# Decoder block on one core: the first norm's root by Ln, Exp and a Newton step, the second ada row in one dot, and the activation's low half ahead of the weight's

## What is computed

```python
mod = silu_c @ w_ada[l] + b_ada[l]                  # 6 vectors of 2048
sh1, sc1, g1, sh2, sc2, g2 = jnp.split(mod, 6, axis=-1)
h = modulate(rms_norm(x, norm1_w[l]), sh1, sc1)     # h*(1+sc1)+sh1
proj = h @ w_in[l]
```

## Time and profile before

| what | value |
|---|---|
| median of 3 runs | 2343.6 us (2343.4 to 2343.84) |
| the profiled execution's own time | 2344.19 us |
| its span | 2342.4 us |
| TensorE busy | 2320.1 us (99%) |
| VectorE busy | 1256.4 us (54%) |
| ScalarE busy | 721.7 us (31%) |
| GpSimd busy | 90.7 us (4%) |
| granted TensorE clock, mean | 0.998 |
| transfers | 327.21 MB, mean 140 GB/s; 388 and 410 GB/s in the first two of 40 slices |

### The profile page before, as it was taken

How to read it: one execution, slowest core, us unless ns; L and a number is a source line. 1 busy time by engine, 2 the same in 40 slices (tenths; PEclk the granted TensorE clock), 3 DMA queues, 4 the chain that set the end, 5 groups by cost and what they waited for, 6 DMA issues and landing times.

```text
span 2342.4 us, 28296 instructions
## 1 busy us (share of the span) xinstructions
PE 2320.1 (99%) x10432; PEld 1891.1 (81%) x10432; DVE 1256.4 (54%) x1577; ACT 721.7 (31%) x1013; POOL 90.7 (4%) x59
## 2 busy tenths in 40 slices
PE   8999999999999999999999999999999999999998
PEld 5578888887888888888888888888888888888887
DVE  8989888866666675633333333333333333333354
ACT  3333333344445322421321321322222222222233
POOL 0011112101010000000000000000000000000000
PEclk9999999999999999999999999999999999999999
DMA  9965767622223573222222222222222222222222
GB/s 388 410 240 205 260 244 261 232 81 81 81 79 106 201 282 122 99 96 93 99 99 98 90 98 98 92 98 97 98 98 90 98 98 96 99 92 98 99 90 99
DMA packets 89575, 327.21 MB, mean 140 GB/s; under 512 B 8625, under 2 KB 9137, under 8 KB 89521
## 3 DMA queue, kind: packets, MB, share of 16 engines
q1 hardware_dynamic: 89232, 326.34, 38.8%
q10 hardware_dynamic: 290, 0.16, 0.0%
HBM read 322.27 MB, written 4.19 MB: 139 GB/s over the span
## 4 chain that ended last, share of the span: by engine, by line
PE 92%; DMA 3%; DVE 2%; issue 1%; ACT 0%; POOL 0%; ACTq 0%; POOLq 0%; DVEq 0%
PE bank L478 29%; PE bank L482 29%; PE bank L479 29%; DMA prob<-ada 3%; PE bank L689 1%; PE bank L655 1%; DVE w_lo L1209 1%; DVE ada_sb L1215 0%; PE bank L680 0%; PE bank L594 0%; PE bank L523 0%; PE bank L535 0%; PE bank L672 0%; PE bank L827 0%; PE bank L633 0%
## 5 line engine op out<-in xcount | busy, mean ns | idle before, releaser
L478 PE MATMUL bank<-act_hi,w_hi 128*128 128x512 f32 x2016 | 790.7, 392 | 0.3 <-ACT w_hi L885 0.3
L479 PE MATMUL bank<-act_lo,w_hi 128*128 128x512 f32 x2016 | 785.3, 390 | 0.0
L885 ACT ACTIVATE w_hi<-raw 128x1024 fp32r<-128x1024 f32 x393 | 415.0, 1056 | 835.4 <-PE bank L482 825.8
L1209 DVE TENSOR_TENSOR w_lo<-raw,w_hi 128x1024 fp32r<-128x1024 f32 x393 | 496.3, 1265 | 293.6 <-ACT w_hi L885 280.1
L482 PE MATMUL bank<-act_hi,w_lo 128*128 128x512 f32 x2016 | 498.2, 389 | 0.1
L478 PEld LDWEIGHTS bank<-act_hi,w_hi 128*128 128x128 f32 x2016 | 378.4, 188 | 81.2 <-ACT w_hi L885 2.3
L482 PEld LDWEIGHTS bank<-act_hi,w_lo 128*128 128x128 f32 x2016 | 378.3, 188 | 79.1 <-DVE w_lo L1209 0.5
L479 PEld LDWEIGHTS bank<-act_lo,w_hi 128*128 128x128 f32 x2016 | 378.7, 188 | 77.9
L478 PE MATMUL bank<-u_hi,w_hi 128*128 128x512 f32 (+1 forms) x1040 | 401.6, 387 | 0.0
L479 PE MATMUL bank<-u_lo,w_hi 128*128 128x512 f32 (+1 forms) x1040 | 400.2, 386 | 0.0
L1631 DVE SCALAR_TENSOR_TENSOR xy<-bank,modr,xy 128x512 f32 (+1 forms) x141 | 105.8, 750 | 412.3 <-PE bank L482 412.3
(11 more groups left out here) (176 smaller groups left out, 1304.7 us busy)
## 6 DMA issues: line engine op xcount, KB each, us to landing
raw<-weights SPq DMA_DIRECT2D x400, 512.0 KB, 3.3
ada_sb<-ada SPq DMA_DIRECT2D x78, 1024.0 KB, 5.1
xy<-x_t SPq DMA_DIRECT2D x16, 512.0 KB, 4.8
prob<-ada SPq DMA_DIRECT2D x8, 1024.0 KB, 10.4
ada<-ada SPq DMA_DIRECT2D x7, 1024.0 KB, 8.7
out<-rows_out SPq DMA_DIRECT2D x8, 512.0 KB, 4.1
ada_sb<-ada SPq DMA_DIRECT2D x4, 512.0 KB, 11.4
decay_sb<-decay SPq DMA_DIRECT2D x8, 256.0 KB, 3.3
```

The source lines that it names most:

```text
L478: pe.matmul(acc, stationary, hi, start=first, stop=False)
L479: pe.matmul(acc, stationary, lo, start=False, stop=False)
L885: nc.scalar.activation(w_hi[:, w], raw[:, r], ACT.Copy).then_inc(hi_ready, 1)
L1209: nc.vector.tensor_tensor(w_lo[:, w], raw[:, r], w_hi[:, w].bitcast(F32), ALU.subtract).then_inc(lo_ready, 1)
```

## The change

Six things change.

1. The root of the first norm. ScalarE loads the table with Ln and Exp once the squares are done, takes Ln of the mean (with epsilon as its bias, read from PSUM) and Exp of -1/2 of that, which is a rough root. VectorE makes one Newton step on it (`first_root`, three small instructions on 128 x 4, each waiting for the one before). `token_mean(1)` on VectorE and `token_root(1)` on GpSimd are gone. The table is still there at k = 9, so the load ahead of the Exp at k = 9 is gone, and the load of SiLU's behind it stays.
2. Row 1 of `w_ada` comes in one transfer and is multiplied in one dot. The count of arrivals per buffer (`ada_place`) follows.
3. The copy of the identity stands between two additions of squares, and no more behind them.
4. For split tiles 2 to 12, `modulated_rest` stands ahead of `rest_w`.
5. For split tile 14, `rest_w` stands ahead of the dot of row 30, and `modulated_rest` behind it.
6. GpSimd sets one more small constant (`ln_eps`).

```diff
-HALF_ROWS = (0, 1, 2 * KT - 1)
+HALF_ROWS = (0, 2 * KT - 1)
...
+            load_table(LN_EXP_SET)
+            act.wait_ge(half_ready, 3)
+            act.wait_ge(mean_done, 1)
+            nc.scalar.activation(tok_r[:], ps_a[:, 0:TB], ACT.Ln, scale=LN_SCALE, bias=ln_eps[:, 0:1]).then_inc(first_ln, 1)
+            act.wait_ge(first_ln, 1)
+            nc.scalar.activation(tok_r[:], tok_r[:], ACT.Exp, scale=-0.5, bias=ln_shift[:, 0:1]).then_inc(first_exp, 1)
             act.wait_ge(vec_landed, 16)
             scale1(0)
...
+            def first_root():
+
+                dve.wait_ge(first_exp, 1)
+                nc.vector.scalar_tensor_tensor(tok_v[:], ps_a[:, 0:TB], NORM_EPS, tok_r[:], ALU.add, ALU.mult)\
+                    .then_inc(first_newton, 1)
+                dve.wait_ge(first_newton, 1)
+                nc.vector.scalar_tensor_tensor(tok_v[:], tok_v[:], -0.5, tok_r[:], ALU.mult, ALU.mult).then_inc(first_newton, 1)
+                dve.wait_ge(first_newton, 2)
+                nc.vector.scalar_tensor_tensor(tok_r[:], tok_v[:], 1.5, tok_r[:], ALU.add, ALU.mult).then_inc(tok_r_ready, 1)
...
+                    if m == 9:
+                        dve.wait_ge(ident_landed, 16)
+                        nc.vector.tensor_copy(ident_r[:], ident_early).then_inc(const_ready, 1)
...
-            dve.wait_ge(ident_landed, 16)
-            nc.vector.tensor_copy(ident_r[:], ident_early).then_inc(const_ready, 1)
             dve.wait_ge(vec_landed, 16)
             dve.wait_ge(silu_ready, 2)
             half_dot(0, 0)
-            token_mean(1)
             dve.wait_ge(silu_ready, 4)
             half_dot(0, 1)
-            half_dot(1, 0)
-            half_dot(1, 1)
+            first_root()
+            dot1(0, 1)
             normed(0, 0)
             rest_w(Count(0))
             modulated_rest(0, 0)
             for k in range(1, KT):
+                if k == KT - 1:
+                    rest_w(Count(k - 1))
                 dot1(k, 0)
                 behind_split = k > 1 and k - 1 in SPLIT
                 if behind_split:
-                    rest_w(Count(k - 1))
                     modulated_rest(0, k - 1)
+                    if k < KT - 1:
+                        rest_w(Count(k - 1))
                     normed(0, k)
...
             nc.gpsimd.memset(minus_half[:], -0.5).then_inc(half_ready, 1)
-            pool.wait_ge(half_ready, 2)
-            token_root(1)
+            nc.gpsimd.memset(ln_eps[:], NORM_EPS * LN_SCALE).then_inc(half_ready, 1)
+            pool.wait_ge(half_ready, 3)
```

## The result

The changed kernel takes 2361.86 us (median of 6 runs, 2361.28 to 2362.49) and the kernel before, beside it, 2343.72 us (6 runs, 2343.4 to 2344.3): a ratio of 1.0079, 95% interval 1.0068 to 1.0089. It is 0.8% slower, where 2343.0 was forecast. The profiled execution took 2361.92 us at a span of 2360.1, 17.7 more than the span of before.

A forecast was written before the change was run, and what follows sets the result against it. Transfers were taken to bound the kernel up to 115.6 us, with TensorE fed behind that. Terms 0, 0, 0 and -0.55 took the profiled 2344.19 to 2343.64 us, a median of about 2343.0, range 2341.9 to 2344.3.

The forecast's parts named there:

- two regimes: Whole kernel: up to 115.6 us work waits for transfers; behind it TensorE is fed and only passes on its start.
- The sum: Whole kernel: profiled 2344.19 us plus four terms, 0, 0, 0 and -0.55, gives 2343.64; median about 2343.0 us.
- The chance of 0.01 for slower: Whole kernel: chance given to a time slower by over 0.2%, left only to what was overlooked.
- The root of the first norm: Kernel start: first normed about 0.8 us earlier, bounds 0.3 to 1.1, lost in the wait for row 4.
- term 0: Kernel start: no time gained, since row 4's arrival stays and its wait grows from 0.54 to about 1.3 us.
- Row 1 and tiles 2 to 12: First phase: one dot saves about 0.15 us and act_lo waits go, yet both terms 0; tiles' bounds 0 to -0.1.
- Tile 14: Last split tile: rest_w fills VectorE's idle gap before row 30's dot; -0.55 us, bounds 0 and -1.14.
- The start's gain: First phase, rival: arrivals follow issues, so the first norm's 0.8 us is kept; 2342.2 us, chance 0.14.
- TensorE does not keep its waits: First phase, rival denied here: TensorE sets the round, so 5.3 us of waits are gained; 2337.8 us, chance 0.02.
- The tail's gap: Tile 14, rival: gap gone because row 30 comes earlier or rest_w is held; 2343.6 us, chance 0.05.
- the fourth rival, the fetch: First phase: the long round's 0.95 us, tied to instruction fetches, falls elsewhere; 2342.1 or 2344.0 us, chance 0.04 each.
- GpSimd's first instruction: q_lo at 130.7, rival: being first costs about 1.0 us more, delaying w_lo; 2344.1 us, chance 0.07.

The follow-up runs named there:

- e1_aligned: All of the change, but the new constant in a spare column of minus_half's tile, so no tile moves; 2343.24 us, ratio 0.9999 to the kernel before.
- e10_norm: Kernel before plus the new first root, row 1 in one dot and moved identity copy, old order of low halves, tiles unmoved; 2343.46 us, ratio 1.0.
- e9_order: Kernel before with only modulated_rest put ahead of rest_w in tiles 2 to 12; 2343.45 us, ratio 1.0.
- e8_tail: Kernel before with only rest_w of tile 14 put ahead of row 30's dot; 2342.91 us, ratio 0.9998.
- e2_shift32: Kernel before with one unused 4-byte tile where the change puts its constant, moving later tiles 32 bytes; 2362.59 us, ratio 1.0081.
- e13_u256: Kernel before with u_hi and u_lo moved by 256 bytes; 2343.64 us, ratio 1.0.
- e3_shift64: Kernel before with an unused 64-byte tile where the change puts its constant, moving later tiles 64 bytes; 2350.07 us, ratio 1.0028.
- e7_u_hi16: Kernel before with u_hi moved by 16 bytes inside a larger tile and u_lo by 128; 2361.16 us, ratio 1.0076.
- e11_u96: Kernel before with u_hi and u_lo moved by 96 bytes; 2363.25 us, ratio 1.0085.
- e5_act32: Kernel before with act_hi and act_lo moved by 32 bytes and everything behind them by 128; 2395.88 us, ratio 1.0224.
- e14_u192: Kernel before with u_hi and u_lo moved by 192 bytes; 2362.82 us, ratio 1.0082.
- e15_w_lo32: Kernel before with w_lo alone moved by 32 bytes and everything behind it by 256; 2364.3 us, ratio 1.009.
- e6_w32: Kernel before with w_hi and w_lo moved by 32 bytes and everything behind them by 128; 2397.03 us, ratio 1.0228.

## Why the prediction was wrong

**What bounds the kernel.** The reading of two regimes held for the first phase. It failed in what it made of the second: "behind it TensorE is fed and only passes on the moment at which it was handed its work". That takes for granted that a product costs the same in both kernels. Its step was 0.233 us instead of 0.227, 3024 times, 19.4 us in all. **This is the step that failed.** The sum lacks a term for where the tiles lie, and of edit 6, one more small constant, it costs neither the instruction nor the tile. The diff shows the new tile as one line. The rows of before could not give its price, since they show only one placement; that `hf`, `u_hi` and `u_lo` are declared behind it could be seen, and none of the rivals was made of it. The chance of 0.01 for slower was too small for a term that nothing had bounded.

**The root of the first norm.** Its path became 1.12 us shorter (forecast 0.8, bounds 0.3 to 1.1, so just above them). From the timeline of after:

```profile
18.85 0.26 ACT L1059 ACTIVATE tok_r<-bank,ln_eps 128x4 f32<-128x4 f32 x1 [2.20 <-PE bank L539]
...
19.47 0.16 DVE L1248 SCALAR_TENSOR_TENSOR tok_v<-bank,tok_r 128x4 f32<-128x4 f32 x1 [0.18 <-ACT tok_r L1061]
...
20.17 2.05 PE L629 MATMUL bank<-ident_r,tok_r 128*128 128x128 f32 x8 [1.43 <-DVE tok_r L1253]
...
22.35 0.75 DVE L1272 SCALAR_TENSOR_TENSOR hf<-xy,amul,bank 128x512 f32<-128x512 f32 x1
```

From the first instruction behind the means to `hf` it is 22.35 - 18.85 = 3.50 us, where it was 22.61 - 17.99 = 4.62. The two on ScalarE take 0.62 with their hops, as forecast; the three of the Newton step and the spread's start take 0.70, where 0.9 had been taken. The means themselves came 0.9 us later in this execution, so `hf` did not start at 21.8; in e1_aligned it did (21.69). The wait for row 4 became 1.05 us (forecast near 1.3), its dot stood at 31.15 (forecast 30.9), and term 0 held.

**Row 1 and tiles 2 to 12.** Term 0 held for both. The waits for `act_lo` went and those for `xy` came, 2.7 us in 6 waits in after, as the prediction had it.

**Tile 14.** Forecast -0.55, measured -0.58. Row 30's dot started without a wait at 115.38, behind `w_lo` at 114.33; the first half of row 31 came at 119.06 on the chain, where 119.75 had been forecast for a row 26 that arrived 0.75 later.

**The rivals.** The start's gain is not kept (row 4's dot in e1_aligned and e10_norm). TensorE does not keep its waits (e9_order: 2338 was the rival's time, 2343.45 was measured). The tail's gap was there to be filled (e8_tail). Of the fourth rival, the fetch, the premise was weak: the prediction read the 0.95 us of the long round as belonging to two instruction fetches, but in e2_shift32, whose first phase is the same program, a round from 76.53 to 89.33 holds two fetches of the same sizes and takes the usual 12.80. What made the one round long, 13.8 us in the kernel before and 13.3 in after by the chain, stays open; it stood at the same place in both. GpSimd's first instruction carries no price: in after its first large one took 1.54 us, and the `w_lo` beside it 2.32, where it was 1.61 and 2.31.

```profile
129.47 1.54 POOL L1823 TENSOR_TENSOR q_lo<-rot_a,q_hi 128x512 fp32r<-128x512 f32 x1 [128.56 <-ACT q_hi L953]
...
129.77 2.32 DVE L1219 TENSOR_TENSOR w_lo<-raw,w_hi 128x1024 fp32r<-128x1024 f32 x1
```

Beside `q_lo`, `w_lo` takes 1.1 us more than its usual 1.22; what holds it up there is not shown.

Without the shift the change was worth what was forecast within what can be measured: e1_aligned took 2343.24 us, forecast 2343.0, kernel before 2343.5. It is the only kernel here that has all of the change and no shift, and it can't be told from the kernel before.

## What to carry to other kernels

A new tile, however small, can change the time of products on the tiles declared behind it: in e2_shift32 an unused one of 4 bytes cost 19.1 us. In a kernel bound by TensorE, count how far each streamed tile starts from its weight tile, and keep to a distance that was measured without a price; here these were the kernel's own (by the count above a multiple of 512 bytes) and 256 bytes more. Put small constants into spare columns, as e1_aligned did, or behind the large tiles (which was not tried). Where a kernel's busy time on TensorE changes while the number of products, the clock and the idle time do not, look at placement first, and test it with an unused tile in the old kernel.

## What the runs showed of the hardware

The step of a product of 128 x 512 in fp32r depends on how far the streamed tile starts from the weight tile: 0.227 us at the distance of the kernel before and at 256 bytes more (e13_u256), and 0.229 at 64 more (e3_shift64), 0.232 at 16 (e7_u_hi16), and 0.233 at 32, 96, 128, 192 and 224 (e2_shift32, e11_u96, e5_act32, e14_u192, e15_w_lo32). That is up to 3% of a product's step. The bytes are by the count from the tile sizes, which no trace shows; the times are measured. When all split products had a bad distance, as in e6_w32, the kernel took 2397.03 us instead of 2343.43. A distance better than 0 was not found among those tried; 160 bytes, and distances below 16, were among those not tried.
